# Pairs of neighbouring expert chunks loaded as one 2 MB transfer in a two-layer diffusion trunk

## The reference, cut to what matters

```python
def _swiglu(h, w_up, w_down):
    g, u = jnp.split(h @ w_up, 2, axis=-1)
    return (jax.nn.silu(g) * u) @ w_down

def _moe(h, w_router, w_up, w_down):
    ...
    top_val, top_idx = lax.top_k(logits, TOP_K)
    ...
    out = jnp.zeros_like(hf)
    for e in range(N_EXPERTS):
        out = out + gates[:, e:e + 1] * _swiglu(hf, w_up[e], w_down[e])
    return out.reshape(B, T, D)
```

## Time and profile before

| | us |
|---|---|
| median of 3 runs | 1743.06 |
| lowest and highest | 1740.35, 1747.47 |
| the profiled execution | 1743.41 |
| its span, first to last instruction | 1741.3 |
| first item, up part | about 911 to 1165 |
| first item, down part | about 1165 to 1300 |
| second item | about 1300 to 1728 |

### The profile page before, as it was taken

The page is one execution under the profiler, slowest core; times in us unless marked ns, Lnnn a source line. Parts: engine busy times, 40 slices in busy tenths (PEclk is TensorE's granted clock), DMA queues, the critical chain, the costliest instruction groups (busy, mean ns, idle before and its releaser), DMA issues.

```text
span 1741.3 us, 28335 instructions
## 1 busy us (share of the span) xinstructions
PE 1638.6 (94%) x11532; PEld 1218.1 (70%) x11532; DVE 873.3 (50%) x1305; ACT 652.4 (37%) x956; POOL 28.7 (2%) x49
## 2 busy tenths in 40 slices
PE   5999999999999999999999999998998999899897
PEld 3886568899999777876766667765556666665564
DVE  2434764899997355743763233333433322323447
ACT  2324663544444333424733233333332322323232
POOL 1200000000000000000010000000000000000000
PEclk8999999999999999999999999999999999999999
DMA  9824863133334545333289999999999999999996
GB/s 349 197 97 171 322 233 97 49 98 98 98 122 157 206 146 172 118 97 121 98 297 408 421 421 410 390 401 416 415 422 420 421 421 420 419 416 417 417 417 257
DMA packets 117440, 481.98 MB, mean 277 GB/s; under 512 B 8218, under 2 KB 52424, under 8 KB 68928
## 3 DMA queue, kind: packets, MB, share of 16 engines
q1 hardware_dynamic: 114720, 472.66, 69.2%
q0 software_dynamic: 2592, 7.51, 2.0%
HBM read 477.27 MB, written 2.87 MB: 276 GB/s over the span
## 4 chain that ended last, share of the span: by engine, by line
PE 68%; DMA 13%; DVE 9%; ACT 5%; issue 5%; SPq 0%; DVEq 0%; ACTq 0%
PE PS L1020 17%; PE PS L1022 16%; PE PS L1021 16%; DMA RAWB<-in_w_exp_up 6%; PE PS L1680 4%; DMA RAWB<-in_w_exp_down 3%; PE PS L1052 3%; ACT BH L2346 2%; PE PS L1752 2%; PE PS L1309 2%; DMA RAWA<-in_w_exp_up 2%; DMA RAWA<-in_w_exp_down 1%; PE PS L1319 1%; PE PS L1331 1%; DVE RAWBL L3277 1%
## 5 line engine op out<-in xcount | busy, mean ns | idle before, releaser
L3277 DVE TENSOR_TENSOR RAWBL<-RAWB,BH 128x2048 fp32r<-128x2048 f32 x45 | 103.1, 2292 | 277.2 <-ACT BH L2346 277.2
L1020 PE MATMUL PS<-HH,WH 128*128 128x256 f32 (+1 forms) x600 | 193.5, 323 | 6.3 <-DVE HL L2577 2.9
L1020 PE MATMUL PS<-BH,HE 128*128 128x512 f32 x448 | 182.1, 406 | 12.6 <-DVE RAWBL L3277 11.8
L1022 PE MATMUL PS<-HH,WL 128*128 128x256 f32 (+1 forms) x600 | 190.6, 318 | 0.0
L1021 PE MATMUL PS<-HL,WH 128*128 128x256 f32 (+1 forms) x600 | 190.6, 318 | 0.0
L3277 DVE TENSOR_TENSOR RAWAL<-RAWA,BH 128x2048 fp32r<-128x2048 f32 x39 | 89.4, 2292 | 197.0 <-ACT BH L2346 196.4
L2346 ACT ACTIVATE BH<-RAWB 128x2048 fp32r<-128x2048 f32 x45 | 86.2, 1915 | 239.9 <-DMA RAWB<-in_w_exp_up 120.0
L1022 PE MATMUL PS<-BH,LE 128*128 128x512 f32 x448 | 175.9, 393 | 0.0
L2538 DVE TENSOR_TENSOR WL<-RAW,WH 128x2048 fp32r<-128x2048 f32 (+1 forms) x41 | 91.7, 2237 | 143.0 <-ACT WH L1950 142.7
L2346 ACT ACTIVATE BH<-RAWA 128x2048 fp32r<-128x2048 f32 x39 | 74.6, 1914 | 204.1 <-DMA RAWA<-in_w_exp_up 129.9
L1950 ACT ACTIVATE WH<-RAW 128x2048 fp32r<-128x2048 f32 (+1 forms) x41 | 76.8, 1874 | 141.4 <-PE PS L1022 141.3
(11 more groups left out here) (398 smaller groups left out, 3147.3 us busy)
## 6 DMA issues: line engine op xcount, KB each, us to landing
RAWB<-in_w_exp_up SPq DMA_DIRECT2D x106, 1024.0 KB, 10.5
RAWA<-in_w_exp_up SPq DMA_DIRECT2D x106, 1024.0 KB, 10.6
RAWA<-in_w_exp_down SPq DMA_DIRECT2D x56, 1024.0 KB, 10.0
RAWB<-in_w_exp_down SPq DMA_DIRECT2D x56, 1024.0 KB, 9.8
RAW<-in_w_mod SPq DMA_DIRECT2D x48, 1024.0 KB, 6.8
RAW<-in_w_ffn_up SPq DMA_DIRECT2D x22, 1024.0 KB, 5.5
RAW<-in_w_in_c SPq DMA_DIRECT2D x12, 1024.0 KB, 5.1
RAW<-in_w_ffn_down SPq DMA_DIRECT2D x10, 1024.0 KB, 7.2
```

The costliest lines, as they stand in the source:

```text
L1020: mm(ps, ah, bh, start=start, stop=False)
L1022: return mm(ps, al, bh, start=False, stop=stop)
L3277: v.tensor_tensor(expert_low(big_place(a, i), i), expert_raw(big_place(a, i), i), BH[:, a % 2, :].bitcast(F32), ALU.subtract).then_inc(s_b ...
```

## The change

The weights of the experts are laid out on the host in pairs of chunks (`in_pairs`): each pair has 128 rows of 16 KB, and a single chunk is one half of each row. The load orders are rewritten so that two neighbouring small chunks of one slot stand next to each other in the ring, and they are issued as one DMA of 2 MB with one semaphore. Chunks of the big expert stay single. The down products go through stages in twos (`small_two`), in the load order and in PE's order. PE's order in the up parts is untouched. ACT's order is untouched, and DVE's only in its last lines.

```diff
+        def pair(j, what, first, second):
+            return [(j, what, *first), (j, what, *second)]
...
+        for st in range(NST):
+            low, high = ((st, 0), (st, 1)), ((st, 2), (st, 3))
+            bigs = [[("big", "u", st, kq)] for kq in range(4)]
+            order += [pair(0, "u", *low), bigs[0], pair(0, "u", *high), bigs[1], pair(1, "u", *low),
+                      pair(1, "u", *high), bigs[2], pair(2, "u", *low), bigs[3], pair(2, "u", *high)]
+        for st0, h in ((0, 0), (2, 0), (4, 0), (1, 1), (3, 1), (5, 1)):
+            smalls = [pair(j, "d", (st0, h), (st0 + 1, h)) for j in range(NS)]
+            bigs = [[("big", "d", st0 + n, h)] for n in range(2)]
...
+            if (st0, h) == (5, 1):
+                order += [smalls[0], *bigs, *smalls[1:]]
+            else:
+                order += [smalls[0], bigs[0], smalls[1], bigs[1], smalls[2]]
...
+        s01, s23 = halves(*SINGLE)
+        wanted = [s01, one(0), s23]
+        for p, (u0, u1) in enumerate(PAIRS[:THREES]):
+            (s01, s23), (t01, t23) = halves(*u0), halves(*u1)
+            a = 1 + 3 * p
+            wanted += [s01, one(a), s23, one(a + 1), t01, one(a + 2), t23]
...
+        r = MRING
+        while wanted:
+            at = 0
+            if r % 4 == 3 and wanted[0] != fixed_pair and len(wanted[0]) == 2:
+                at = [len(o) for o in wanted].index(1)
+            item = wanted.pop(at)
...
             def load_experts(i, phase, qs=range(CPI)):
...
+                    if leader(q, i) != q:
+                        continue
...
-                    if not isinstance(i, int) or ring_of(q, i) >= MRING:
-                        sp.wait_ge(*chunk_used(ring_before(q, i), i))
+                    both = q in (joined1 if isinstance(i, int) else joined)
+                    if not isinstance(i, int):
+                        sp.wait_ge(*chunk_used(last_of_two(q) if both else ring_before(q, i), i))
+                    else:
+                        for n in (q, q + 1) if both else (q,):
+                            if ring_of(n, i) >= MRING:
+                                sp.wait_ge(*chunk_used(ring_before(n, i), i))
...
+                    ring = (RAWB if slot < 4 else RAWA)[:, slot % 4:slot % 4 + 1 + both, :]
...
                     def down(more):
...
+                        small_two(1, 5, 0, more)
+                        big_down(1, 5, more)
+                        small_two(1, 5, 1, more)
+                        big_down(1, 6, more)
+                        small_down(1, 5, 2, more)
+                        if not more:
...
+                            scatter_last(0)
+                        small_down(1, 6, 2, more)
...
                 big_last(0)
+                big_last(1)
                 dve.wait_ge(*small_used(NS - 1, "d", NST - 1, 1, i))
...
-                big_last(1)
```

More of the change, by code:

```diff
@@ L231, in trunk @@
         THREES = 5
[L232 to L245, removed]
+        places = [[(0, "u", st, kq)] for st in range(LEAD) for kq in range(4)]
+        def halves(st, j):
+            return pair(j, "u", (st, 0), (st, 1)), pair(j, "u", (st, 2), (st, 3))
@@ new lines, in trunk @@
+        fixed_pair = halves(LEAD, 0)[0]
+        r = MRING
[4 more added lines that the diff above has]
+            item = wanted.pop(at)
+            if item != fixed_pair:
+                assert r % 4 + len(item) <= 4
+                r += len(item)
+            places.append(item)
+        joined1 = {sum(len(o) for o in places[:n]) for n, o in enumerate(places) if len(o) == 2 and o != fixed_pair}
@@ L246, in trunk @@
+        order1 = [o for group in places for o in group]
+        assert [o[0] == "big" for o in order1[-MRING:]] == [o[0] == "big" for o in order[len(order1) - MRING:len(order1)]]
+        UPS = len(order1)
         assert 1 + 3 * THREES == 4 * 4 and len(PAIRS) - THREES == NST - 4
@@ L817, in expert_low, with leader, led @@
             return RAWBL[:, slot, :] if slot < 4 else RAWAL[:, slot - 4, :]
+        def leader(q, i):
+            return q - 1 if q - 1 in (joined1 if isinstance(i, int) else joined) else q
+        def led(qs, slot, i):
+            return sum(leader(n, i) == n and not (isinstance(i, int) and n in aside) and ring_of(n, i) % MRING == slot
+                       for n in qs)
         def expert_landed(q, i):
@@ L823, in expert_landed @@
                 return s_aside[n], 16 * before + 16
-            r = ring_of(q, i)
-            return s_mland[r % MRING], i * (16 * CPI // MRING) + 16 * (r // MRING + 1)
+            n = leader(q, i)
+            slot = ring_of(n, i) % MRING
+            if isinstance(i, int):
+                return s_mland[slot], 16 * led(range(n + 1), slot, i)
+            first, up, down = (led(range(UPS), slot, 0), led(range(UPS), slot, None), led(range(UPS, CPI), slot, None))
+            before = first + (led(range(UPS, n + 1), slot, None) if n >= UPS
+                              else led(range(n + 1), slot, None) - up)
+            return s_mland[slot], i * (16 * (up + down)) + 16 * before
         def ring_before(q, i):
@@ L843, in chunk_used, with last_of_two @@
             return s_sused, i * SPI + (ahead * SPI + smalls.index(q) + 1)
+        def last_of_two(q):
+            two = q - MRING, q + 1 - MRING
+            bigs = [n for n in two if n % CPI in big_at]
+            return bigs[0] if bigs else two[1]
         def big_place(a, i):
@@ L1903, in down @@
[L1903 to L1909 removed]
+                            small_two(0, st, 1, more)
+                            if more and st == 4:
+                                gather(1)
```

103 lines of the change are left out of this document (62 added, 41 removed).

## The result

| | before | changed |
|---|---|---|
| median, us | 1743.23 (4 runs) | 1798.26 (4 runs) |
| lowest and highest | 1740.35, 1747.47 | 1791.83, 1800.23 |
| span of the profiled execution | 1741.3 | 1798.1 |

The ratio is 1.0308, with a 95% interval of 1.0288 to 1.0328. The changed kernel is 55 us slower by the medians, 54 by the ratio. The direction of the forecast holds; its size, +23 us, is less than half of what came.

What follows compares the result with a forecast made beforehand. PE was taken to bound the first item's up part, transfers everything after. Terms 9 + 13 + 5 + 4 - 8 = +23 us on the 1741.3 span, plus small allowances, gave 1767 us; 8-in-10 range 1749 to 1789.

Steps and rivals of the forecast that it cites:

- Part 1: Fewer, longer rows: 0.11 us gained per pair on 78 pairs of the second item and first down part; -8 us.
- it doesn't do what it says: Rival: a 16 KB row runs as two of 8 KB, rate stays 421 GB/s; 1775 us, chance 0.2.
- Part 2: First item's up part: late big-chunk slots hold the loads behind them in SP's queue; +22 us in sum.
- first hold: First item's up part: B03 waits for B01's slot, pair 1u10 1u11 stands behind it, PE waits; +9.0 us.
- the carrying on of the first hold: Later first-item up rounds: delay passed on, 6.5 us over rounds 2 to 5, 6.5 over the last three.
- The rule for one late load: Landing is the later of previous landing and issue + 3.1 us, plus 2.49 for each chunk.
- at least 3.9 us between issue and previous landing, so no gap: Steady up stages of the second item: pairs are issued early enough that transfers never pause.
- Part 3: Down parts and junctions: pairs waiting for late slots leave transfer gaps; +5 us together.
- Part 4: Kernel's end: B5 lands two places later, PE waits 2.7 us, last small chunk ends later; +4 us.
- Loads win: Rival: first item's gaps absorbed and rate rises more than forecast, so faster; 1741 to 1748 us, chance 0.07.
- a wash: Rival: only the 9 us wait at 1u10 stays; 1754 us, or 1748 with junctions covered; chance 0.13.
- Starvation: Rival: late issues everywhere cost like the slow one at 1095.3; 1785 to 1795 us, chance 0.15.

Runs made afterwards that it cites:

- natural: Kernel before, its orders kept, only small chunks already side by side joined (14 pairs first item, 28 second): 1741.27 us, ratio 0.999.
- late_old: Changed kernel with the last three rounds of the first item's up part loaded singly in the old order: 1785.3 us, ratio 1.0246.
- early_old: Changed kernel with the first five rounds of the first item's up part loaded singly in the old order: 1774.32 us, ratio 1.0169.
- singles: Changed kernel's orders with no transfer joined, every chunk its own 1 MB load: 1786.42 us, ratio 1.0253.
- filler: Changed kernel with useless matmuls in PE's waits, at 1u10 and in the second item's up stages from stage 2: 1787.95 us, ratio 1.0247.
- up2_old: Changed kernel with the second item's up part loaded singly in the old order: 1791.48 us, ratio 1.0281.
- down_old: Changed kernel with both down parts as before in loads, PE's order and DVE's last lines: 1779.67 us, ratio 1.0213.
- layout: Kernel before, its orders and 1 MB transfers kept, only the weights in the new paired layout: 1745.15 us, ratio 1.0009.
- split: Changed kernel, first item's up part: pairs beginning in slot 3 or 7 issued as singles, no big chunk drawn forward: 1778.23 us, ratio 1.0201.

## Why the prediction was right or wrong

**The bound** was right. PE sets the pace in the first item's up part and the transfers behind it; both had little to spare, and the kernel had no room for late loads.

**Part 1, -8.** Right in kind, a little too large. A pair lands 4.90 us behind the previous load when the queue is full, where two singles take 4.97 (medians of the landings): 0.07 us, or 5 us for 78 pairs; `natural` shows 0.07 too. The rival "it doesn't do what it says" is out, since 424 GB/s stand against 420. The page "DMA: Bandwidth & Descriptors" of the Trainium skill (Rules for kernel authors) says to coalesce many small transfers into large ones. From 1 MB to 2 MB, with the order held fixed, that won about 2 us here (ratio 0.9977 to 1.0002), and with the order bent for it the kernel lost 55.

**Part 2, first hold, +9.0.** Right, in place, cause and size: 8.62 us, with SP at B03 3.3 us later than forecast because PE was (the 3 us told above). The steps behind it were too small. Up to the last round of three I had 15.5 us and it became 23 (20 without those 3); the last three rounds had 6.5 and took 12.5. So the part is 35.7 us behind where the sum had 22. The step that failed is the carrying on of the first hold. For the last three rounds it had one transfer gap in each, of 2 to 4 us. The trace has eight, 19 us in sum beyond the transfers, and four of these are pairs issued with a slack of 0 to 2 us, at 2.5 to 3.5 us each. The rule for one late load was right (3.1 us from issue to transfer; 2.8 to 3.5 in the rows above). What I misjudged is how many loads are late: twelve issues in the part, seven of them single big chunks whose slots were freed late, and five of them pairs, which wait for the later of two slots. `late_old` measures 13 us there, `early_old` 24 for the rounds before, and `singles` shows that joining adds to it.

**The price of the clock** is missing from the prediction, which let PE go on at full speed after each wait. In the first item's up part PE was busy 13 us longer for the same work; how much of that is on the path isn't settled. On the second item it is: I gave its up part gaps of nothing and 5 us of gain in rate, and it grew by 3.0 us in length, and 5.5 in lag. The sentence "at least 3.9 us between issue and previous landing, so no gap" holds at full clock, for the last big chunk of a stage to within 0.4 us: that is what the filler shows (3.5 to 4.0). In the changed kernel it came to 2.1 to 3.7, and there were gaps. The sentence did not look at PE's wait at the small transposes, which the spacing of the big chunks sets, nor at what a wait does to the matmuls behind it, and so to the slots that they free. `filler` and `up2_old` both take out 6.7 us by their traces (3 to 7, as said above).

**Part 3, +5.** The item's boundary was forecast at 2.4 and the lag grew by 3.8. The first pair of the second half was right: a gap of 1.5 us where I had 1.6. What I had too small is the rest of the down parts: the lag grows by 2.2 us over the first item's and by 5.2 over the second's. The second item's has 1.6 us of gap at B3 of its first half, issued 1.4 us ahead of the previous landing, 1.3 at the pair behind it, and smaller ones elsewhere. The three growths are 11.2 us, after the gain in rate (36 pairs of the down parts at 0.07, 2.5 us), so near 14 where I had 5.

**Part 4, +4.** Right in size, and in part by luck: the last landing lags 52.4 us and the end 56.8, so 4.4. The chain of waits near the end, beside the earlier trace rows: B5, two small chunks, B6, one, the scatter, one.

```profile
1760.50 1.92 ACT BH L2435
...
1766.01 0.49 PE PS L1088
...
1773.34 1.85 PE PS L1820 x16
...
1780.90 0.99 PE PS L1820 x8
...
1783.03 0.99 PE PS L1820 x8
```

B5 landed at 1760.4 and starts on PE 5.6 us later, as forecast, behind a wait of 2.8 (forecast 2.7). But its product takes 7.3 us and not 5.7, since the clock is at 0.5 behind that wait, and the landings behind B5 have gaps of about 1 us, which gives the end about as much back against the last landing. Neither is in the prediction.

```profile
1766.90:1770.30 3.40, 3.40 (x10) 2.61 (x9) 3.24 (x4) 0.00 (x0) 0.00 (x0) 0.50 1.03 434
```

**The sum.** By landings: the first item's up part 35.7 us (forecast 22), the down parts and the boundary 11.2 (5, less 3 of gain in rate), the second item's up part 5.5 (a gain of 5), the end 4.4 (4); 56.8 where the sum had 23. Of the 34 us that are missing, 14 are the carrying on, 11 the second item's up part and 9 the down parts.

**The rivals.** *Loads win* and *a wash* are out. *Starvation*, 1785 to 1795 with a chance of 0.15, came nearest, but its cause is not the one given: B03, issued late, took 5.3 us from issue to landing, not 7.7. It was many late loads, not slower ones. The range ended at 1789; its upper bound took ten gaps at 2 us more, and both missing terms, the clock and the further late loads, lay outside it.

What stays open: how much of the first item's 33 us is the clock; which of the three things that `down_old` undoes makes the down parts longer; and why four of the traces (the changed kernel, `layout`, `split` and `filler`) show a low clock near 910, ahead of anything that differs.

## What to carry to other kernels

A joined load is worth what the longer row saves, here 0.07 us on 5, and it pays only if the neighbours already stand side by side; moving chunks to make neighbours cost 43 us here, since every load behind one that is drawn forward waits in the same in-order queue. Before moving a load, write down for each load how long before the previous landing its slot comes free; below about 3 us it is late (2.8 to 3.5 us passed here from issue to transfer), and a late pair holds up two chunks. And cost a wait of TensorE twice: once for its length, once for the matmuls behind it if they run at half the clock, as they did after six of seven waits of 2.2 us and more in the second item's up part.

## What the runs showed of the hardware

- Rows of 16 KB land a pair in 4.90 us, two singles of 8 KB rows take 4.97; no difference is seen between a pitch of 8 and of 16 KB (ratio 1.0009, 0.9996 to 1.0022).
- TensorE's granted clock fell to 0.5 (1.2 GHz) for 3.4 or 6.8 us behind waits of PE (2.2 to 4.1 us in the second item's up part, six times out of seven; 8.6 in the first item). With useless matmuls in the waits the low stretches of the second item's up part went from 20.5 to 3.4 us, and the whole kernel was 10 us faster.
- A load issued on a nearly empty queue landed after 5.3 us for 1 MB and 8.2 to 8.4 us for 2 MB: some 3 us ahead of the transfer (2.5 and 4.9 us) in both cases.
